# Prompt attention in another order of query blocks: 1, 8, 2, 7, 3, 6, 4, 5, with early and late blocks in pairs

## The chip, the core and the metric

The kernel runs on one core of one Trainium2 chip. The metric is the device time of one execution in microseconds (us). Five engines work side by side, each with a queue of its own in program order: TensorE (PE in the profile; its weight loads have a row of their own, PEld), VectorE (DVE), ScalarE (ACT), GpSimd (POOL) and SyncE (SP, which issues DMAs). They wait for one another by semaphores alone.

## The reference, cut to what matters

One layer of a streaming encoder: a SwiGLU feed-forward half step, a token mixer (a recurrent branch and an attention branch side by side), a second feed-forward half step and a final norm, for one prompt of 1024 tokens and eight running streams of 16 tokens. The change touches the attention of the prompt alone: 16 heads of width 64, causal, with a bias from summed forget gates.

```python
for blk in range(s_len // Q_BLOCK):                    # 8 blocks of 128 queries
    q0, q1 = blk * Q_BLOCK, (blk + 1) * Q_BLOCK
    s = einsum('bqhd,bkhd->bhqk', q[:, q0:q1], k[:, :q1]) * scale
    s = s + ft[:, :, q0:q1, None] - ft[:, :, None, :q1]
    p = softmax(where(causal, s, -inf))
    outs.append(einsum('bhqk,bkhd->bqhd', p, v[:, :q1]))
```

The n-th block of queries sees n blocks of 128 keys, so the eight blocks of a head have 1 to 8 key blocks, 36 in all. They do not depend on each other.

## The kernel before, in words

All matmuls that need float32 accuracy are done in a split form: a value is kept as a high part and a low part (the rest), and products of the parts are summed. In the prompt attention the probabilities are split into `pT_hi` and `pT_lo` (views of `w_hi` and `w_lo`), and the values tile `vs_[hh]` holds high and low columns beside each other, 128 in all.

Heads go in pairs: `PAIRS` = 8 rounds of a loop, each of 16 steps `k`, 8 for each of the two heads (`hh`). Step `k` handles query block `qi = k % 8`. Every engine has its own program for the same steps, written out by hand:

- **PE** (`att_tensor`), at step k: `scores` of step k+2 (L2212 and L2213, pieces of up to 512 keys against the high and the low part of k; then one 128-column matmul with the causal mask, L2214), into one of two score areas of two PSUM banks; `turn` of step k (L2227), which transposes the probabilities in units of up to four key blocks, one unit to a PSUM bank, banks 4 and 5 in turn; and half of `values` (L2246): in even steps the pass with `pT_hi`, in odd steps that with `pT_lo`, for the pair of query blocks that was finished by the step before. A pair of blocks (before: 2j and 2j+1) shares one output bank of 256 columns, so that a key block which both see is one matmul of 256 moving columns, and one that only the later block sees is one of 128 columns (`q0`).
- **DVE** (`att_vector`): `maxima` of step k+2 (L2419, adds the bias and takes the row extreme), `lows` of step k (L2435, a turned unit minus its high part, one for each unit), `output` (L2444, a pair's result to SBUF) and, at one step of a head, the reciprocal of the row sums (L2449) and its copy `rec_out` (L2424).
- **ACT** (`att_scalar`): `exp` of step k+1 (L2295), then the copies of step k's units to `pT_hi` (L2312); after step 1 of each head also `split_head_hi` (L2282, L2283), two copies of 1024 columns that round the next head's k and q.
- **POOL** (`att_gpsimd`): the low parts of the next head's k and q (L2334, L2337), the split of the values (L2346, L2348), and the sum, scaling and split of the finished heads (L2355, L2361, L2378, L2380).
- **SP** (`att_sync`): loads of k, q, v and bias for the heads to come, the store and reload of the inverse row sums, the move of one half of a head's output.

The waits that matter below: `turn` of a unit waits until the unit two before it has been read by `lows` (semaphore `pa_l`), since it overwrites that bank; it also waits for `exp` of its step (`pa_exp`). `scores` wait for `maxima` two steps earlier (`pa_max`), and at a head's first step for POOL's split (`pa_split`). `values` wait for the copies or lows of both blocks of the pair, and for `output` of the pair two before. The number of units before each step is a table, `UNITS_BEFORE`, and a head has 12 units in either order.

Of the kernel before, what the change touches and what calls it, by code (L numbers as in the profile page):

```python
# [58 lines left out]
def program(nc, ctx, a, o):  # L59
# [5 lines left out]
    def sem(name):  # L65
        if name not in S:
            S[name] = ctx.enter_context(nc.semaphore(name))
        return S[name]
# [2041 lines left out]
    PAIRS = H // 2  # L2110
    STEPS = 16
    QUARTERS = 8
    UNITS_BEFORE = (0, 1, 2, 3, 4, 6, 8, 10)
    HEAD_UNITS = 12
    vs_ = [v[:].rearrange("p (k n) -> p k n", n=128) for v in vs]
    pT_hi = [w[:].rearrange("p (k n) -> p k n", n=256) for w in w_hi[0:2]]
# [2 lines left out]
    def units_of(i, k):  # L2119

        first = i * 2 * HEAD_UNITS + (HEAD_UNITS * (k // 8) + UNITS_BEFORE[k % 8])
        return [(first + n, 4 * n, min(4 * n + 4, k % 8 + 1)) for n in range(k % 8 // 4 + 1)]

    def bank_of(k, n):
        return 4 + (UNITS_BEFORE[k % 8] + n) % 2
# [73 lines left out]
    def att_tensor(eng):  # L2199

        def scores(i, k):
            hh, qi = k // 8, k % 8
            keys = 128 * (qi + 1)
            if qi == 0:
                eng.wait_ge(sem("pa_split"), i * 2 + hh + 2)
            eng.wait_ge(sem("pa_max"), i * 16 + k - 2 + 1 + 16)
            lhs = q_hl[hh][:, 128 * qi:128 * qi + 128]
            for c0 in range(0, keys, 512):
                c1 = min(c0 + 512, keys)
                out = psum[:, 1024 * (k % 2) + c0:1024 * (k % 2) + c1]  # L2210

                eng.matmul(out, lhs, k_hi[hh][:, c0:c1], start=True, stop=False)  # L2212
                last = eng.matmul(out, lhs, k_lo[hh][:, c0:c1], start=False, stop=c1 < keys)  # L2213
            last = eng.matmul(psum[:, 1024 * (k % 2) + keys - 128:1024 * (k % 2) + keys], ident_r[:], causal_r[:],  # L2214
                              start=False, stop=True)
            last.then_inc(sem("pa_s"), 1)

        def turn(i, k, first):

            eng.wait_ge(sem("pa_exp"), i * 16 + k + 1)  # L2220
            for n, (e, k0, k1) in enumerate(units_of(i, k)):
                eng.wait_ge(sem("pa_l"), e - 1 + 2)
                if k == 10 or (k == 2 and not first):
                    eng.wait_ge(sem("pa_rec"), i * 2 + k // 10 + 2)
                    eng.transpose(ps[bank_of(k, n)][0:8, 384:512], srec[:, 1 - k // 10, :], ident[:])
                for kb in range(k0, k1):
                    last = eng.transpose(ps[bank_of(k, n)][:, 128 * (kb - k0):128 * (kb - k0) + 128],  # L2227
                                         pr[k % 4][:, 128 * kb:128 * kb + 128], ident[:])
                last.then_inc(sem("pa_t"), 1)

        def values(i, q, low):

            j, hh = q % 4, q // 4
            done = i * 2 * HEAD_UNITS + (HEAD_UNITS * hh + (UNITS_BEFORE + (HEAD_UNITS,))[2 * j + 2])
            if not low:
                if j == 0:
                    eng.wait_ge(sem("v_split"), i * 4 + 2 * hh + 2)
                eng.wait_ge(sem("pa_o"), i * 8 + q - 2 + 1 + 2)
                eng.wait_ge(sem("pa_h"), done)
            else:  # L2240
                eng.wait_ge(sem("pa_l"), done + 2)
            probs = (pT_lo if low else pT_hi)[q % 2]
            n = 2 * j + 2
            for kb in range(n):
                q0 = 128 if kb == n - 1 else 0
                last = eng.matmul(ps[6 + q % 2][:, q0:256], vs_[hh][:, kb, :], probs[:, kb, q0:256],  # L2246
                                  start=(not low and kb == 0), stop=(low and kb == n - 1))
            last.then_inc(sem("pa_vl" if low else "pa_vh"), 1)

        def body(i, first=False, last=False):  # L2250
            for k in range(STEPS):
                if k + 2 < STEPS:
                    scores(i, k + 2)
                elif not last:
                    scores(i + 1, k + 2 - STEPS)
                turn(i, k, first)
                if k >= 2:
                    values(i, (k - 2) // 2, k % 2 == 1)
                elif not first:
                    values(i - 1, QUARTERS - 1, k == 1)  # L2260

        eng.wait_ge(sem("br_free"), 20)
        scores(0, 0)
        eng.wait_ge(sem("br_free"), 22)
        scores(0, 1)
        eng.wait_ge(sem("br_free"), 24)
        eng.wait_ge(sem("state_out_ready"), 2)
        body(0, first=True)
        with eng.Fori(1, PAIRS - 1) as i:
            body(i)  # L2270
        body(PAIRS - 1, last=True)
        values(PAIRS - 1, QUARTERS - 1, False)
        values(PAIRS - 1, QUARTERS - 1, True)
        eng.wait_ge(sem("pa_rec"), 2 * PAIRS + 2)
        eng.wait_ge(sem("pa_l"), PAIRS * 2 * HEAD_UNITS + 2)
        eng.transpose(ps[4][0:8, 384:512], srec[:, 1, :], ident[:]).then_inc(sem("last_rec_turned"), 1)
# [8 lines left out]
    def att_scalar(eng):  # L2285
        eng.wait_ge(sem("br_full"), 24)
        eng.activation(acts_hi[:, :, TP:T], att_s[:], ACT.Copy).then_inc(sem("a_hi"), 1)

        def exp(i, k):
            hh, qi = k // 8, k % 8  # L2290
            keys = 128 * (qi + 1)
            if qi == 0:
                eng.wait_ge(sem("pa_rec"), i * 2 + hh - 1 + 2)
            eng.wait_ge(sem("pa_max"), i * 16 + k + 1 + 16)
            eng.activation(pr[k % 4][:, 0:keys], pr[k % 4][:, 0:keys], ACT.Exp, bias=stat[:, k % 4, 0:1], scale=-1.0,  # L2295
                           accum_out=ssum[:, hh, qi:qi + 1]).then_inc(sem("pa_exp"), 1)

        def body(i, first=False, last=False):
            if first:
                exp(i, 0)  # L2300
            for k in range(STEPS):
                if k + 1 < STEPS:
                    exp(i, k + 1)
                elif not last:
                    exp(i + 1, 0)
                hh, qi = k // 8, k % 8
                q = k // 2
                for n, (e, k0, k1) in enumerate(units_of(i, k)):
                    eng.wait_ge(sem("pa_t"), e + 1)
                    if not (first and q < 2):  # L2310
                        eng.wait_ge(sem("pa_vh"), i * 8 + q - 1)
                    eng.activation(pT_hi[q % 2][:, k0:k1, 128 * (qi % 2):128 * (qi % 2) + 128],  # L2312
                                   ps[bank_of(k, n)][:, 0:128 * (k1 - k0)].rearrange("p (k n) -> p k n", n=128),
                                   ACT.Copy).then_inc(sem("pa_h"), 1)
                if k == 1:
                    split_head_hi(eng, i, i * 2 + 1, 1)
                if k == 9 and not last:
                    split_head_hi(eng, i, i * 2 + 2, 0)
                if k == 13 and last:
                    eng.wait_ge(sem("v_split"), 4 * PAIRS)  # L2320
                    eng.wait_ge(sem("pa_s"), 16 * PAIRS + 16)
                    split_hi(eng, B_BRA, BRA_FIRST_SLOT, BRA_RAWS[0])
        body(0, first=True)
        with eng.Fori(1, PAIRS - 1) as i:
            body(i)
        body(PAIRS - 1, last=True)
        last = PAIRS - 1
        eng.wait_ge(sem("pair_scaled"), PAIRS + 1)
        eng.activation(acts_hi[:, last, 0:TP], lw[:], ACT.Copy).then_inc(sem("pair_hi"), 1)
# [74 lines left out]
    def att_vector(eng):  # L2404
# [5 lines left out]
        eng.wait_ge(sem("states_stored"), 64)  # L2410

        def maxima(i, k):
            hh, qi = k // 8, k % 8
            keys = 128 * (qi + 1)
            eng.wait_ge(sem("pa_s"), i * 16 + k + 1 + 16)
            if qi == 0:
                eng.wait_ge(sem(f"kbias_loaded{hh}"), i * 16 + 16)
            eng.memset(wait_marks[:, k % 4:k % 4 + 1], 0.0)
            eng.tensor_tensor_reduce(pr[k % 4][:, 0:keys], psum[:, 1024 * (k % 2):1024 * (k % 2) + keys],  # L2419
# [4 lines left out]
            eng.tensor_copy(rec_rows[:], bank[0:8, 384:512]).then_inc(sem("rec_moved"), 1)  # L2424

        def lows(i, k, first):
            qi, q = k % 8, k // 2
            for n, (e, k0, k1) in enumerate(units_of(i, k)):
                eng.wait_ge(sem("pa_h"), e + 1)
                if not (first and q < 2):  # L2430
                    eng.wait_ge(sem("pa_vl"), i * 8 + q - 1)
                if k == 10 or (k == 2 and not first):
                    rec_out(i * 2 + k // 10 - 1, ps[bank_of(k, n)])
                cols_ = slice(128 * (qi % 2), 128 * (qi % 2) + 128)
                eng.tensor_tensor(pT_lo[q % 2][:, k0:k1, cols_],  # L2435
                                  ps[bank_of(k, n)][:, 0:128 * (k1 - k0)].rearrange("p (k n) -> p k n", n=128),
                                  pT_hi[q % 2][:, k0:k1, cols_].bitcast(F32), ALU.subtract).then_inc(sem("pa_l"), 1)
# [1 line left out]
        def output(i, q, first=False):  # L2439
            hh, j = q // 4, q % 4  # L2440
            eng.wait_ge(sem("pa_vl"), i * 8 + q + 1)
            if j == 0 and not first:
                eng.wait_ge(sem("pair_added"), i * 2 + hh - 1)
            eng.tensor_copy(ou[hh][:, 256 * j:256 * j + 256], ps[6 + q % 2][:, 0:256]).then_inc(sem("pa_o"), 1)  # L2444

        def inverse(i, hh):
            hd = i * 2 + hh
# [320 lines left out]
```

## Time and profile before

| what | value |
|---|---|
| median of 3 runs | 3396.83 us (3395.95 to 3397.89) |
| the profiled execution | 3401.43 us, span of its instructions 3399.6 us |
| PE busy | 3269.5 us (96% of the span) |
| DVE, ACT, POOL busy | 1260.7, 986.6, 916.5 us |
| prompt attention, within the span | about 2046 to 2323 us |
| in it: PE, ACT, DVE, POOL busy | 242, 217, 212, 193 us of 277 |
| mean granted TensorE clock | 0.985 |

Starts are microseconds from the first instruction of the profiled execution. A row of a timeline gives the start, the duration, the engine, the source line, the operation, the output tile and the inputs, the shape, and how many instructions in a row were merged (x8); in square brackets how long the engine sat idle ahead of it, and who ended the wait. The starts of PE's matmuls and of its weight loads (PEld) are what the argument uses; the ends of matmuls are modelled.

### The profile page before, as it was taken

What the parts mean: (1) busy time and instruction counts of PE and PEld (TensorE: products, weight loads), DVE (VectorE), ACT (ScalarE), POOL (GpSimd) and SP (SyncE); (2) the same over time, 40 slices, a digit from 0 to 9 for tenths busy, and PEclk for the clock granted to TensorE, in tenths of its full rate; (3) what the DMA queues carried; (4) which work ended last, traced back from release to release, by engine and by line L of the source; (5) the groups of instructions that cost most, each with busy time, mean ns of one, the idle gap of its engine ahead of it and who ended that gap; (6) DMA issues with size and microseconds to landing.
All of it is one profiled execution on the core that took longest, in us unless ns stands there. A gap on an engine that the chain in (4) does not pass through costs nothing.

```text
span 3399.6 us, 53111 instructions
## 1 busy us (share of the span) xinstructions
PE 3269.5 (96%) x20617; PEld 3113.2 (92%) x20617; DVE 1260.7 (37%) x2587; ACT 986.6 (29%) x1577; POOL 916.5 (27%) x474
## 2 busy tenths in 40 slices
PE   7999999999998999999999998889999999999997
PEld 4899999999988999998877897879989999999997
DVE  5322222222267343541222316775343222333225
ACT  4111111111253233233434407873232111111114
POOL 2222222222331111111111025773133222322223
PEclk8999999999999999999999999999999999999999
DMA  6223222221121321326767745555211111111101
GB/s 220 87 95 102 89 87 98 86 88 60 38 83 35 113 84 63 107 77 230 265 213 270 258 138 136 139 140 177 96 38 63 37 37 37 37 49 37 58 17 56
DMA packets 247038, 351.80 MB, mean 103 GB/s; under 512 B 31885, under 2 KB 182981, under 8 KB 246658
## 3 DMA queue, kind: packets, MB, share of 16 engines
q1 hardware_dynamic: 220482, 316.87, 29.2%
q10 hardware_dynamic: 26432, 33.18, 2.7%
q8 instruction: 90, 1.47, 0.2%
q14 instruction: 34, 0.28, 0.0%
HBM read 297.74 MB, written 48.07 MB: 102 GB/s over the span
## 4 chain that ended last, share of the span: by engine, by line
PE 86%; DVE 5%; issue 3%; ACT 3%; SPq 1%; DMA 1%; POOL 1%; ACTq 0%; DVEq 0%; POOLq 0%
PE psum L304 25%; PE psum L308 25%; PE psum L307 25%; PE psum L1753 2%; PE psum L2227 1%; PE psum L489 1%; PE psum L2246 1%; PE psum L1800 1%; DVE w_lo L2435 1%; PE psum L1394 1%; PE psum L1767 1%; DVE acts_lo L830 1%; DVE h_f L785 1%; PE psum L496 1%; PE psum L2212 1%
## 5 line engine op out<-in xcount | busy, mean ns | idle before, releaser
L304 PE MATMUL psum<-acts_hi,w_hi 128*128 128x384 f32 x4032 | 1392.9, 345 | 10.8 <-issue 9.2
L308 PE MATMUL psum<-acts_hi,w_lo 128*128 128x384 f32 x4032 | 1357.6, 337 | 0.0
L307 PE MATMUL psum<-acts_lo,w_hi 128*128 128x384 f32 x4032 | 1357.2, 337 | 0.0
L304 PEld LDWEIGHTS psum<-acts_hi,w_hi 128*128 128x128 f32 x4032 | 760.4, 189 | 48.4 <-issue 31.2
L294 POOL TENSOR_TENSOR w_lo<-w_raw,w_hi 128x2048 fp32r<-128x2048 f32 x106 | 491.0, 4639 | 1148.1 <-ACT w_hi L288 1148.1
L307 PEld LDWEIGHTS psum<-acts_lo,w_hi 128*128 128x128 f32 x4032 | 760.7, 189 | 4.4 <-issue 0.9
L308 PEld LDWEIGHTS psum<-acts_hi,w_lo 128*128 128x128 f32 x4032 | 759.5, 188 | 0.0
L1116 DVE TENSOR_TENSOR u_f<-psum,gated 128x384 f32<-128x384 f32 x132 | 73.6, 558 | 1014.5 <-ACT gated L1010 1014.5
L1066 POOL TENSOR_TENSOR u_lo<-u_f,u_hi 128x384 fp32r<-128x384 f32 x132 | 134.4, 1018 | 928.5 <-ACT u_hi L1015 928.5
L1188 DVE SCALAR_TENSOR_TENSOR x<-psum,mods,x 128x384 f32<-128x384 f32 (+1 forms) x552 | 314.6, 570 | 183.7 <-PE psum L308 183.7
L288 ACT ACTIVATE w_hi<-w_raw 128x2048 fp32r<-128x2048 f32 x106 | 200.5, 1910 | 560.7 <-PE psum L304 535.1
L304 PE MATMUL psum<-u_hi,w_hi 128*128 128x384 f32 x1056 | 356.3, 337 | 3.4 <-DVE x L1193 2.2
L308 PE MATMUL psum<-u_hi,w_lo 128*128 128x384 f32 x1056 | 355.6, 337 | 0.0
L307 PE MATMUL psum<-u_lo,w_hi 128*128 128x384 f32 x1056 | 355.5, 337 | 0.0
L1010 ACT ACTIVATE gated<-psum 128x384 f32<-128x384 f32 x132 | 64.8, 491 | 892.7 <-PE psum L308 892.6
L304 PEld LDWEIGHTS psum<-u_hi,w_hi 128*128 128x128 f32 x1056 | 199.0, 188 | 4.9 <-DVE x L1193 3.3
L307 PEld LDWEIGHTS psum<-u_lo,w_hi 128*128 128x128 f32 x1056 | 198.9, 188 | 0.3
L308 PEld LDWEIGHTS psum<-u_hi,w_lo 128*128 128x128 f32 x1056 | 199.1, 189 | 0.0
L1967 DVE COPY kTs<-psum 128x512 f32<-128x512 f32 x64 | 44.3, 692 | 251.1 <-PE psum L1753 251.1
L2227 PE MATMUL psum<-ident,pr 128*128 128x128 f32 x576 | 92.8, 284 | 32.0 <-DVE w_lo L2435 27.8
L2435 DVE TENSOR_TENSOR w_lo<-psum,w_hi 128x512 fp32r<-128x512 f32 (+1 forms) x192 | 100.4, 551 | 27.3 <-ACT w_hi L2312 26.5
L2227 PEld LDWEIGHTS psum<-ident,pr 128*128 128x128 f32 x576 | 63.3, 142 | 46.8 <-DVE w_lo L2435 29.8
(261 smaller groups left out, 2978.7 us busy)
## 6 DMA issues: line engine op xcount, KB each, us to landing
w_raw<-in_ffn_w SPq DMA_DIRECT2D x66, 1024.0 KB, 5.2
kc<-in_cache_k SPq DMA_DIRECT2D x32, 1024.0 KB, 7.0
vc<-in_cache_v SPq DMA_DIRECT2D x16, 2048.0 KB, 7.9
w_raw<-in_w_ada SPq DMA_DIRECT2D x28, 1024.0 KB, 5.0
w_raw<-in_w_in SPq DMA_DIRECT2D x28, 1024.0 KB, 5.1
sp<-sample_bias SPq DMA_DIRECT2D x128, 65.0 KB, 2.6
ada_w<-in_w_ada SPq DMA_DIRECT2D x4, 2048.0 KB, 13.4
w_raw<-in_w_ada_f SPq DMA_DIRECT2D x8, 1024.0 KB, 5.7
```

The costliest lines, as they stand in the source:

```text
L288: eng.activation(w_hi[st][:], w_raw[raw][:], ACT.Copy).then_inc(sem("w_hi_done"), 1)
L294: eng.tensor_tensor(w_lo[st][:], w_raw[raw][:], w_hi[st][:].bitcast(F32), ALU.subtract).then_inc(sem("w_lo_done"), 1)
L304: pass1 = eng.matmul(out, whi, ahi, start=first, stop=False)
L307: eng.matmul(out, whi, alo, start=False, stop=False)
L308: return eng.matmul(out, wlo, ahi, start=False, stop=last)
L1010: eng.activation(gated[n % 2][:], ps[2 * (n % 2)][:, 0:CH], ACT.Silu).then_inc(sem("gated_ready"), 1)
L1066: eng.tensor_tensor(u_lo[:, t, tokens_of(c)], u_f[n % 2][:], u_hi[:, t, tokens_of(c)].bitcast(F32), ALU.subtract).then_inc(sem("u_lo_done" ...
L1116: eng.tensor_tensor(u_f[n % 2][:], ps[2 * (n % 2) + 1][:, 0:CH], gated[n % 2][:], ALU.mult).then_inc(sem("u_free"), 1)
L1188: last = eng.scalar_tensor_tensor(xt[:, d, t0:t0 + cp], bank[:, 0:cp], mods[:, gate, d, 0:1], xt[:, d, t0:t0 + cp], ALU.mult, ALU.add)
L1753: last = eng.transpose(ps[TURNED][:, 128 * m:128 * m + 128], kc[:, 4 * half + m, 128 * p:128 * p + 128], ident[:])
L2227: last = eng.transpose(ps[bank_of(k, n)][:, 128 * (kb - k0):128 * (kb - k0) + 128], pr[k % 4][:, 128 * kb:128 * kb + 128], ident[:])
L2435: eng.tensor_tensor(pT_lo[q % 2][:, k0:k1, cols_], ps[bank_of(k, n)][:, 0:128 * (k1 - k0)].rearrange("p (k n) -> p k n", n=128), pT_hi[q % ...
```

## The change

`BLOCKS` gives the query block of each of a head's eight steps: 0, 7, 1, 6, 2, 5, 3, 4 (counted from 0). Two steps in a row are a pair, now an early and a late block: 1 and 8 key blocks, 2 and 7, 3 and 6, 4 and 5. `UNITS_BEFORE` follows from the order. In `values` the key blocks that both see are those up to the early block; all further ones are matmuls of 128 columns. `output` writes its two blocks to two separate places. The number of steps, of units, of transposes, of score matmuls and the positions of all other work in the steps stay. The diff, without lines that only rename an index:

```diff
-    UNITS_BEFORE = (0, 1, 2, 3, 4, 6, 8, 10)
+    BLOCKS = (0, 7, 1, 6, 2, 5, 3, 4)
+    UNITS_BEFORE = tuple(sum(qi // 4 + 1 for qi in BLOCKS[:n]) for n in range(8))
...
-        return [(first + n, 4 * n, min(4 * n + 4, k % 8 + 1)) for n in range(k % 8 // 4 + 1)]
+        qi = BLOCKS[k % 8]
+        return [(first + n, 4 * n, min(4 * n + 4, qi + 1)) for n in range(qi // 4 + 1)]
...
         def scores(i, k):
-            hh, qi = k // 8, k % 8
+            hh, qi = k // 8, BLOCKS[k % 8]
             keys = 128 * (qi + 1)
-            if qi == 0:
+            if k % 8 == 0:
                 eng.wait_ge(sem("pa_split"), i * 2 + hh + 2)
...
             probs = (pT_lo if low else pT_hi)[q % 2]
-            n = 2 * j + 2
+            early, late = BLOCKS[2 * j], BLOCKS[2 * j + 1]
+            n = late + 1
             for kb in range(n):
-                q0 = 128 if kb == n - 1 else 0
+                q0 = 128 if kb > early else 0
                 last = eng.matmul(ps[6 + q % 2][:, q0:256], vs_[hh][:, kb, :], probs[:, kb, q0:256],
                                   start=(not low and kb == 0), stop=(low and kb == n - 1))
...
         def exp(i, k):
-            hh, qi = k // 8, k % 8
+            hh, qi = k // 8, BLOCKS[k % 8]
...
         def maxima(i, k):
-            hh, qi = k // 8, k % 8
+            hh, qi = k // 8, BLOCKS[k % 8]
...
-            eng.tensor_copy(ou[hh][:, 256 * j:256 * j + 256], ps[6 + q % 2][:, 0:256]).then_inc(sem("pa_o"), 1)
+            early, late = BLOCKS[2 * j], BLOCKS[2 * j + 1]
+            out = ou[hh][:].rearrange("p (b n) -> p b n", n=128)[:, early:late + 1:late - early, :]
+            eng.tensor_copy(out, ps[6 + q % 2][:, 0:256].rearrange("p (b n) -> p b n", n=128)).then_inc(sem("pa_o"), 1)
```

## Rows read from the trace of the kernel before

**Rows 1.** Busy us (count) of PE, PEld, DVE, ACT, POOL by stretch; granted clock, DMA.

```profile
2046.00:2323.00 277.00, 242.23 (x1744) 219.15 (x1745) 212.24 (x672) 216.83 (x480) 192.65 (x98) 0.98 0.54 129
...
2323.00:2700.00 377.00, 368.17 (x2083) 365.70 (x2082) 147.35 (x262) 81.93 (x121) 112.25 (x52) 0.99 0.26 87
```

**Rows 2.** Timeline of PE's matmuls in one head and the start of the next.

```profile
2182.17 0.98 PE L2227 MATMUL psum<-ident,pr 128*128 128x128 f32 x7 [0.65 <-DVE w_lo L2435]
...
2191.80 0.65 PE L2227 MATMUL psum<-ident,pr 128*128 128x128 f32 x4
...
2194.80 0.33 PE L2227 MATMUL psum<-ident,pr 128*128 128x128 f32 x1 [0.82 <-DVE w_lo L2435]
...
2198.84 0.98 PE L2227 MATMUL psum<-ident,pr 128*128 128x128 f32 x7 [0.66 <-DVE w_lo L2435]
```

**Rows 3.** Who waited for whom, 2084 to 2300 us: total, times, longest.

```profile
PEld psum L2227 <- DVE w_lo L2435: 28.4, 37, 1.1
...
PEld psum L2227 <- issue: 3.0, 14, 0.8
```

**Rows 4.** Instructions by line and shape, 1900 to 2700 us: count, busy us, mean ns.

```profile
L2246 PE MATMUL psum<-w_lo,vs 128*128 128x256 f32 x256 | 46.3, 303 | 0.0
...
L2246 PE MATMUL psum<-w_lo,vs 128*128 128x128 f32 x64 | 14.4, 224 | 0.0
```

**Rows 5.** Timeline of PE's weight loads, one for each matmul.

```profile
2181.07 0.19 PEld L2213 LDWEIGHTS psum<-k_lo,q_hl 128*128 128x128 f32 x1
2181.18 0.19 PEld L2214 LDWEIGHTS psum<-causal_r,ident_r 128*128 128x128 f32 x1
...
2184.41 0.89 PEld L2227 LDWEIGHTS psum<-ident,pr 128*128 128x128 f32 x8 [0.40 <-DVE w_lo L2435]
...
2186.48 0.14 PEld L2227 LDWEIGHTS psum<-ident,pr 128*128 128x128 f32 x1
2186.68 1.01 PEld L2246 LDWEIGHTS psum<-w_hi,vs 128*128 128x128 f32 x8
```

**Rows 6.** PE's matmuls in one scores piece, behind a piece of 512 columns.

```profile
2189.66 0.40 PE L2213 MATMUL psum<-k_lo,q_hl 128*128 128x512 f32 x1
2189.90 0.22 PE L2212 MATMUL psum<-k_hi,q_hl 128*128 128x128 f32 x1
2189.95 0.27 PE L2213 MATMUL psum<-k_lo,q_hl 128*128 128x128 f32 x1
```

**Rows 7.** Timeline of ACT: two copies of a step, then the split stretch.

```profile
2182.94 0.98 ACT L2312 ACTIVATE w_hi<-psum 128x512 fp32r<-128x512 f32 x2 [0.15 <-PE psum L2227]
...
2188.97 1.05 ACT L2282 ACTIVATE k_hi<-kf 128x1024 fp32r<-128x1024 f32 x1
...
2190.86 0.71 ACT L2295 ACTIVATE pr<-pr,stat 128x512 f32<-128x512 f32 x1
...
2191.57 0.48 ACT L2312 ACTIVATE w_hi<-psum 128x384 fp32r<-128x384 f32 x1
```

**Rows 8.** Timeline of DVE, the low part of the same step.

```profile
2192.39 0.54 DVE L2435 TENSOR_TENSOR w_lo<-psum,w_hi 128x384 fp32r<-128x384 f32 x1
```

**Rows 9.** Instructions by line and shape again, of ACT and DVE.

```profile
L2435 DVE TENSOR_TENSOR w_lo<-psum,w_hi 128x512 fp32r<-128x512 f32 x96 | 64.5, 686 | 22.1 <-ACT w_hi L2312 21.5
...
L2312 ACT ACTIVATE w_hi<-psum 128x512 fp32r<-128x512 f32 x96 | 55.3, 593 | 21.3 <-PE psum L2227 20.8
...
L2295 ACT ACTIVATE pr<-pr,stat 128x896 f32<-128x896 f32 x16 | 16.7, 1046 | 0.0
```

**Rows 10.** Whole timeline: POOL's q split, and scores of the next head.

```profile
2193.51 2.38 POOL L2337 TENSOR_TENSOR q_hl<-qf,q_hl 64x1024 fp32r<-64x1024 f32 x1
...
2197.69 0.27 PE L2212 MATMUL psum<-k_hi,q_hl 128*128 128x128 f32 x1
```

**Rows 11.** Timeline of PE at the last two steps of the last head.

```profile
2314.58 0.95 PE L2227 MATMUL psum<-ident,pr 128*128 128x128 f32 x7 [1.02 <-DVE w_lo L2435]
...
2318.11 1.06 PE L2227 MATMUL psum<-ident,pr 128*128 128x128 f32 x8 [1.93 <-DVE w_lo L2435]
```

More of the change, by code:

```diff
@@ L2289, in exp @@
         def exp(i, k):
-            hh, qi = k // 8, k % 8
+            hh, qi = k // 8, BLOCKS[k % 8]
             keys = 128 * (qi + 1)
-            if qi == 0:
+            if k % 8 == 0:
                 eng.wait_ge(sem("pa_rec"), i * 2 + hh - 1 + 2)
@@ L2311, in body @@
                         eng.wait_ge(sem("pa_vh"), i * 8 + q - 1)
-                    eng.activation(pT_hi[q % 2][:, k0:k1, 128 * (qi % 2):128 * (qi % 2) + 128],
+                    eng.activation(pT_hi[q % 2][:, k0:k1, 128 * (k % 2):128 * (k % 2) + 128],
                                    ps[bank_of(k, n)][:, 0:128 * (k1 - k0)].rearrange("p (k n) -> p k n", n=128),
@@ L2412, in maxima @@
         def maxima(i, k):
-            hh, qi = k // 8, k % 8
+            hh, qi = k // 8, BLOCKS[k % 8]
             keys = 128 * (qi + 1)
             eng.wait_ge(sem("pa_s"), i * 16 + k + 1 + 16)
-            if qi == 0:
+            if k % 8 == 0:
                 eng.wait_ge(sem(f"kbias_loaded{hh}"), i * 16 + 16)
@@ L2426, in lows @@
         def lows(i, k, first):
-            qi, q = k % 8, k // 2
+            q = k // 2
             for n, (e, k0, k1) in enumerate(units_of(i, k)):
@@ L2433, in lows @@
                     rec_out(i * 2 + k // 10 - 1, ps[bank_of(k, n)])
-                cols_ = slice(128 * (qi % 2), 128 * (qi % 2) + 128)
+                cols_ = slice(128 * (k % 2), 128 * (k % 2) + 128)
                 eng.tensor_tensor(pT_lo[q % 2][:, k0:k1, cols_],
```

## The prediction

> **What bounds the kernel now.** I read the busy times by stretch first, then the prompt attention alone. TensorE works nearly without a break in the stretches around it, 368 of 377 us in the one that follows, but 242 of 277 us within it [rows 1]; whatever the attention gains or loses is thus passed on to the end. The granted clock is 0.98 there and 0.99 in the next stretch, both near the level of 2.4 GHz [rows 1], so it plays no part. PE's timeline is periodic: the same seven transposes begin at 2182.17 and at 2198.84, so a head takes 16.67 us [rows 2]. The waits of the weight loads, PE's front edge, say how much of this is idle: 28.4 us for DVE's `lows` and 3.0 us for what the profile calls issue, in 216 us [rows 3]. That is 31.4 / 216 x 16.67 = 2.42 us for a head. The rest, 14.25 us, is work in program order. The longest waits, 0.65 to 0.82 us, are where PE wants a turned bank (4 or 5) that DVE has not read yet [rows 2]. DVE and ACT are busy for 212 and 217 of 277 us [rows 1]: no engine is full, PE is nearest to it, and the gaps come from round trips PE, ACT, DVE, PE.
>
> The new order can win at most those 2.42 us a head, 38.7 us over 16 heads, less what it adds.
>
> **What it adds: six more matmuls in each pass.** Before, the pairs have 2, 4, 6 and 8 key blocks; one pass over a head is 16 matmuls of 256 columns and 4 of 128, as the counts 256 and 64 over 16 heads say [rows 4]. After, the pairs have 8, 7, 6 and 5 key blocks, of which 1, 2, 3 and 4 are shared: 10 of 256 columns and 16 of 128. The columns are the same, 16 x 256 + 4 x 128 = 10 x 256 + 16 x 128 = 4608; the matmuls, and with them the weight loads, go from 20 to 26.
>
> Which of the two is paid? Eight value matmuls load their weights within 1.01 us, the last load of 0.19 included, so one follows the next after 0.82 / 7 = 0.117 us. Two loads for 128-column matmuls in a row (2181.07, 2181.18) stand 0.11 us apart [rows 5]. So halving the columns saves 0.007 us, not half. A 128-column matmul starts 0.05 us behind another only where the one ahead of both was long (2189.66, 2189.90, 2189.95) and the weights were there early [rows 6]; a long run of them is nearer to the first case. With 0.11: before 16 x 0.117 + 4 x 0.11 = 2.31 us a pass, after 10 x 0.117 + 16 x 0.11 = 2.93. That is 0.62 a pass, 1.24 a head (two passes), 19.8 us in all. The lower bound is 0, if columns alone counted; the upper one is 6 x 0.117 x 2 x 16 = 22.5 us.
>
> The Trainium skill (TensorE: Matmul & The Clock Gate, LDWEIGHTS) gives a weight load's time as its columns over 1.2, 107 ns for 128, whatever the rows; the 0.11 us agree, and by this rule the change costs PE time. Another rule of that page (Back-to-back issue gap) puts a stream of load and matmul pairs at 81 ns for 128 columns, against the 0.11 measured here; by it the added work, with 12 more such matmuls in each of two passes, would be 1.24 - 24 x 0.03 = 0.52 us a head.
>
> **What it moves: where PE waits.** Prices first. Four transposes: the eight loads of 0.89 less a single one of 0.14, over 7, give 0.107 each, 0.43 for four [rows 5]. Scores: a 512-column piece takes 0.24 (2189.66 to 2189.90), so 0.06 a block, at least 0.11 a matmul, twice for high and low, and 0.11 for the mask [rows 5, 6]: 0.33, 0.35, 0.47, 0.59, 0.81, 0.83, 0.95 us for 1 to 7 blocks. Passes after: 0.89, 0.78, 0.68, 0.58 for 8, 7, 6, 5 blocks. A bank's round trip: the first half of the seven transposes ends at 2182.17 + 0.43 = 2182.60, and the bank is used again at 2184.41, 1.81 us later [rows 2, 5]; its pieces, 0.34 to the copy, 0.59, 0.69 and some 0.05 of handing over, make 1.67 [rows 7, 9].
>
> Units now come 1, 2, 1, 2, ... by step. I walked one head through and compared, at each place where PE needs something, PE's own work since then with the time until it is there. Four places are not covered.
>
> (A) Step 3. After the first half of block 8 is turned (step 1), ACT needs 0.34 to begin, 0.98 for two copies, 1.89 for the split of the next head (2188.97 to 2190.86), then `exp` of seven key blocks, 0.71 + (1.046 - 0.713) = 1.04, and 0.23 until PE begins (2191.57 to 2191.80) [rows 2, 7, 9]: 4.48 us. PE has the other half 0.43, the 5-block pass 0.58, scores of 3 blocks 0.47, the turn of step 2 with the inverse 0.32, the 8-block pass 0.89, scores of 6 blocks 0.83: 3.52. It waits 0.96. Before, ACT had one copy ahead of the split at this place, and an `exp` of four blocks behind it.
>
> (B) Step 3, second half. Its bank frees when step 2's copy and low part are done, which stand behind that `exp` on ACT. Before, copy, inverse and low part took from 2191.57 to 2192.39 + 0.54, 1.36 us for three blocks [rows 7, 8]; for two about 1.15 (an estimate: two instructions a block shorter, 0.1 each). PE arrives after 0.23 + 0.43: a wait of 0.49.
>
> (C) Step 6. Covered: 0.21 + 0.78 + 0.33 = 1.32 of a bank's trip. DVE is free there, so 1.67 is taken: 0.35, at most 0.49.
>
> (D) Step 0 of the next head. Covered: 0.11 + 0.68 + 0.35 = 1.14; DVE has `maxima` of block 8 ahead of the second half, so 1.81 is taken: 0.67, at least 0.53.
>
> Together 2.47 us (2.33 to 2.61) in place of 2.42. The waits do not go, they move. So a head grows by 1.24 + 0.05 = 1.29 us, 16 heads by 20.6. The ends give back about 1: the last head waits 1.02 and 1.93 us behind ACT's weight split today [rows 11], and its last `exp` has five blocks instead of eight, 3 x 0.11 less; the start, one long scores piece earlier, I bound by 1 us either way.
>
> **Edits at no cost.** `maxima`, `exp`, copies and `lows` have the same shapes and counts a head. `output` still moves 256 columns, on DVE, which has room. The waits that moved from `qi == 0` to `k % 8 == 0` guard the same steps. SP's and POOL's instructions keep their places. The split starts later in a head, after two copies and eight blocks: 0.11 + 0.58 + 0.95 + 0.43 + 0.34 + 0.98 = 3.39 us from the head's first turn against 2.49 before (2186.48 to 2188.97) [rows 5, 7]. POOL's low part of q ended at 2195.89, 1.8 us ahead of the next head's scores [rows 10]; these come 11.2 us after the head's first turn today, and after the change 12.6: scores of 7, 3, 6, 4 and 5 blocks 3.65, 27 blocks turned and the inverse 3.00, six passes 4.50, (A) and (B) 1.45. So the slack grows by 0.5; if this cover went, each us would cost 16.
>
> **The sum.** On the profiled execution, 3401.43 us (span 3399.6), +20.6 - 1 = 3421; it stood 4.6 above the median of the runs, so 3396.8 + 19 = 3416 us.
>
> **Rivals.** (1) The evening-out works and the bank waits go, as a pair of steps now weighs the same wherever it stands; for it speaks that ACT and DVE have a fifth of their time free, against it the 0.96 us of (A), a sum of ACT work in queue order. It decides where a head's waits fall below 2.42 - 1.24 = 1.18 us; with none left the time is (1.24 - 2.42) x 16 = -19: 3378. Chance 0.09. (2) Waits fall by half and pay for the loads, within 0.2% (6.8 us, about what a measurement of this kernel can tell from no change): 3390 to 3403, 0.10. (3) Matmuls of 128 columns run at 0.06: no work added, but where PE's work covered a trip the wait takes it back, 0.05 for each of 1 + 7 in (A), 5 in (C), 3 in (D), 0.8 us. A head grows by 0.85, in all 13 less 1: 3409. Against it stands the 0.11; 0.08. With the 81 ns of the Trainium skill's page (TensorE: Matmul & The Clock Gate, Back-to-back issue gap) the same reckoning gives 0.52 + 0.05 + 0.48 = 1.05 a head, 3413. (4) POOL's split comes late after all, 1 us a head on top: 3432, 0.03. The forecast itself has 0.70, with 3405 to 3426.
>
> Slower: 0.70 + 0.08 + 0.03 = 0.81; same 0.10; faster 0.09. The range is 3400 to 3428: the forecast's own, case 3, and half of case 2; upward the longest trips (2.61 for 2.47, +2) and loads at 0.117 (+3), with as much again for places that I missed.
>
> **What would show it.** The period of a head near 18 us instead of 16.67; 160 matmuls of 256 and 256 of 128 columns in the low pass, 0.11 apart; waits of the turn's weight loads near 2.4 us a head, the longest at step 3, behind `exp`, none on scores for POOL. Wrong would be it if the loads of 128-column matmuls stand closer, or if the wait behind ACT's split does not appear.

## The result, and the profile after

The changed kernel takes 3407.49 us (median of 9), the kernel before 3398.51 in the runs beside it: a ratio of 1.0029, 95% interval 1.002 to 1.0038. A second series gave 3409.63 and 1.0028 (1.0018 to 1.0038). So it is slower, by 9 to 11 us, where 19 were forecast. The time lies in the range, and just beyond the 0.2% that the prediction took as no change.

The period of a head is read from the reciprocal of its row sums, which DVE computes once in each head. Two such rows, ten heads apart, in the timeline of DVE, kernel before:

```profile
2121.23 0.19 DVE L2449 RECIPROCAL srec<-ssum 128x8 f32<-128x8 f32 x1
...
2288.10 0.19 DVE L2449 RECIPROCAL srec<-ssum 128x8 f32<-128x8 f32 x1
```

And after:

```profile
2119.80 0.19 DVE L2453 RECIPROCAL srec<-ssum 128x8 f32<-128x8 f32 x1
...
2295.89 0.19 DVE L2453 RECIPROCAL srec<-ssum 128x8 f32<-128x8 f32 x1
```

That is 16.69 us a head before and 17.61 after, 0.92 more; the prediction had 1.29. A second profile of each kernel gave 16.69 and 17.61 again.

Value matmuls by shape, after, as in [rows 4]:

```profile
L2249 PE MATMUL psum<-w_lo,vs 128*128 128x128 f32 x256 | 35.7, 262 | 0.0
...
L2249 PE MATMUL psum<-w_lo,vs 128*128 128x256 f32 x160 | 34.7, 315 | 0.0
```

The waits of the turn's weight loads, 2084 to 2310 us, as in [rows 3]:

```profile
PEld psum L2229 <- DVE w_lo L2437: 17.0, 36, 0.6
...
PEld psum L2229 <- issue: 8.8, 15, 0.7
...
PEld psum L2227 <- issue: 1.7, 7, 0.3
...
PEld psum L2227 <- DVE w_lo L2437: 1.1, 6, 0.2
```

Together 28.6 us in 226, 2.23 us a head, against 2.42 before (a single wait for `exp`, 0.6 us after and 0.3 before, is left out of both). The rest of a head is 15.38 us against 14.27.

One head in PE's timeline, after, as in [rows 2], from step 0 to step 3:

```profile
2188.83 0.33 PE L2229 MATMUL psum<-ident,pr 128*128 128x128 f32 x1 [0.43 <-DVE w_lo L2437]
2189.03 0.80 PE L2249 MATMUL psum<-w_hi,vs 128*128 128x256 f32 x5
2189.66 0.45 PE L2214 MATMUL psum<-k_hi,q_hl 128*128 128x512 f32 x1
...
2193.02 1.08 PE L2249 MATMUL psum<-w_hi,vs 128*128 128x256 f32 x8
2193.94 0.45 PE L2214 MATMUL psum<-k_hi,q_hl 128*128 128x512 f32 x1
...
2195.36 0.65 PE L2229 MATMUL psum<-ident,pr 128*128 128x128 f32 x4 [0.45 <-ACT pr L2298]
2196.31 0.55 PE L2229 MATMUL psum<-ident,pr 128*128 128x128 f32 x3 [0.30 <-DVE w_lo L2437]
```

The weight loads of the same head, whose waits are PE's front edge, with the eight loads of the 8-block pass:

```profile
2188.82 0.14 PEld L2229 LDWEIGHTS psum<-ident,pr 128*128 128x128 f32 x1 [0.58 <-DVE w_lo L2437]
...
2192.68 0.08 PEld L2227 LDWEIGHTS psum<-ident,srec 128*8 128x8 f32 x1 [0.26 <-issue]
...
2192.99 0.97 PEld L2249 LDWEIGHTS psum<-w_hi,vs 128*128 128x128 f32 x8
...
2195.35 0.42 PEld L2229 LDWEIGHTS psum<-ident,pr 128*128 128x128 f32 x4 [0.59 <-issue]
...
2196.31 0.31 PEld L2229 LDWEIGHTS psum<-ident,pr 128*128 128x128 f32 x3 [0.54 <-DVE w_lo L2437]
...
2202.10 0.42 PEld L2229 LDWEIGHTS psum<-ident,pr 128*128 128x128 f32 x4 [0.25 <-DVE w_lo L2437]
```

All four places of the prediction are there: (D) at 2188.82, (A) at 2195.35, (B) at 2196.31, (C) at 2202.10. A fifth is new: 0.26 us at step 2 (2192.68), inside the stretch over which (A) was counted. Together they make 2.22 us.

ACT in the same stretch: two copies of block 8, the split, `exp` of seven blocks, and only then the copy of step 2:

```profile
2191.23 1.09 ACT L2314 ACTIVATE w_hi<-psum 128x512 fp32r<-128x512 f32 x2 [1.14 <-PE psum L2229]
2192.21 1.06 ACT L2285 ACTIVATE k_hi<-kf 128x1024 fp32r<-128x1024 f32 x1
2193.16 1.06 ACT L2286 ACTIVATE q_hl<-qf 128x1024 fp32r<-128x1024 f32 x1
2194.10 1.04 ACT L2298 ACTIVATE pr<-pr,stat 128x896 f32<-128x896 f32 x1
...
2195.13 0.38 ACT L2314 ACTIVATE w_hi<-psum 128x256 fp32r<-128x256 f32 x1
```

And DVE, which waits 2 us for that copy:

```profile
2195.65 0.28 DVE L2426 COPY rec_rows<-psum 8x128 f32<-8x128 f32 x1 [2.00 <-ACT w_hi L2314]
2195.85 0.40 DVE L2437 TENSOR_TENSOR w_lo<-psum,w_hi 128x256 fp32r<-128x256 f32 x1
```

So the profile looks as forecast, a little smaller. What it cannot say is whether the head is longer for the loads or for the order: the prediction put 1.24 of its 1.29 us on the loads.

### The profile page after: what moved, and what is told of

Its sections match the earlier page's. It is cut to its first block, busy times and chain, and to the rows that moved or that the text cites. A ratio compares the mean times of both kernels' runs of the same rounds, so it can differ in the third digit from the quotient of the medians.

```text
span 3404.5 us, 53491 instructions
## 1 busy us (share of the span) xinstructions
PE 3285.7 (97%) x20809; PEld 3128.6 (92%) x20809; DVE 1260.8 (37%) x2587; ACT 986.3 (29%) x1577; POOL 916.7 (27%) x474
## 4 chain that ended last, share of the span: by engine, by line
PE 88%; DVE 5%; ACT 3%; issue 1%; SPq 1%; DMA 1%; POOL 1%; ACTq 0%; DVEq 0%; POOLq 0%
PE psum L304 25%; PE psum L308 25%; PE psum L307 25%; PE psum L2249 2%; PE psum L2229 2%; PE psum L1753 2%; PE psum L489 1%; PE psum L1800 1%; PE psum L1394 1%; PE psum L1767 1%; DVE acts_lo L830 1%; PE psum L2214 1%; DVE w_lo L2437 1%; PE psum L2215 1%; DVE h_f L785 1%
## 5 line engine op out<-in xcount | busy, mean ns | idle before, releaser
L2437 DVE TENSOR_TENSOR w_lo<-psum,w_hi 128x128 fp32r<-128x128 f32 (+2 forms) x192 | 100.6, 550 | 35.7 <-ACT w_hi L2314 35.2
L2314 ACT ACTIVATE w_hi<-psum 128x128 fp32r<-128x128 f32 (+2 forms) x192 | 88.8, 488 | 62.6 <-PE psum L2229 62.6
```

Source lines behind the costliest of these rows:

```text
L2314: eng.activation(pT_hi[q % 2][:, k0:k1, 128 * (k % 2):128 * (k % 2) + 128], ps[bank_of(k, n)][:, 0:128 * (k1 - k0)].rearrange("p (k n) -> ...
L2437: eng.tensor_tensor(pT_lo[q % 2][:, k0:k1, cols_], ps[bank_of(k, n)][:, 0:128 * (k1 - k0)].rearrange("p (k n) -> p k n", n=128), pT_hi[q % ...
```

## The experiments

All times are medians beside runs of the kernel before on the same chip; a head is the mean over ten heads, read as above.

| kernel | us | ratio to before (95%) | a head, us |
|---|---|---|---|
| g1_before_again (the kernel before) | 3399.25 | 1.0001 (0.9992 to 1.0010) | 16.69 |
| g2_after_again (the changed kernel) | 3409.63 | 1.0028 (1.0018 to 1.0038) | 17.61 |
| e1_cut | 3400.32 | 1.0005 (0.9996 to 1.0014) | 16.93 |
| e2_fewer | 3403.84 | 1.0018 (1.0009 to 1.0027) | 17.27 |
| e3_new_split0 | 3404.76 | 1.0018 (1.0009 to 1.0027) | 16.97 |
| e4_old_split0 | 3388.23 | 0.9973 (0.9962 to 0.9983) | 15.99 |
| f1_old_split0_late | 3388.68 | 0.9968 (0.9956 to 0.9981) | 15.99 |
| f2_new_split0_late | 3399.90 | 1.0004 (0.9995 to 1.0013) | 16.98 |
| f3_new_split0_fewer | 3394.00 | 0.9986 (0.9977 to 0.9995) | 16.40 |
| f4_order_0213 | 3387.05 | 0.9967 (0.9954 to 0.9979) | 15.74 |
| g3_old_split0_cut | 3393.81 | 0.9986 (0.9977 to 0.9995) | 16.44 |

Two theories stand against each other. L: the six further matmuls of a pass are paid wherever they stand. W: PE works into waits for a bank or for ACT, so that added work costs little, and the order costs by its waits.

**The loads alone (e1_cut).**

```diff
-            for kb in range(n):
-                q0 = 128 if kb == n - 1 else 0
+            halved = range(1, 1 + (0, 2, 2, 2)[j])
+            for kb in range(n):
+                parts = [(128, 256)] if kb == n - 1 else [(0, 128), (128, 256)] if kb in halved else [(0, 256)]
+                for q0, q1 in parts:
...
```

> The old order, with six of the 256-column value matmuls of each pass cut into two of 128 (two in each of the three longer pairs): 26 matmuls a pass, 10 of 256 and 16 of 128 columns, as in the changed kernel. Nothing else changes. Theory L (the loads are the cost, wherever they stand): a head grows by 1.24 us, the kernel by 19 to 20 us, as after the change or more. Theory W (what PE gets to do while a bank's trip is open anyway costs little): a pass of the long pairs stands right ahead of the waits for a bank, so most of it is hidden; a head grows by 0.3 us, from 16.69 to about 17.0, the kernel by 5 us, and the waits for the bank fall by 0.9 us a head.

The timeline of DVE and the waits of this kernel, 2090 to 2300 us:

```profile
2117.84 0.19 DVE L2451 RECIPROCAL srec<-ssum 128x8 f32<-128x8 f32 x1
...
2287.09 0.20 DVE L2451 RECIPROCAL srec<-ssum 128x8 f32<-128x8 f32 x1
```

```profile
PEld psum L2227 <- DVE w_lo L2437: 21.9, 37, 1.1
PEld psum L2227 <- issue: 0.5, 1, 0.5
```

A head grows by 0.24 us of the 1.24, the kernel by 2 us, which the interval does not tell from nothing. The waits fall from 2.42 to 22.4 / 210 x 16.93 = 1.81 us a head. Theory L is out for the old order: there the loads are mostly hidden.

**The order alone (e2_fewer).**

```diff
-            n = late + 1
+            n = late + 1 - (2, 2, 1, 1)[j]
```

> The new order and pairs, but each pass leaves out its last six 128-column matmuls (two in the first and second pair, one in the third and fourth), so that it has 20 matmuls as before; the last key blocks do not enter the output. Theory L: a head gets back 1.3 us, the kernel stands about 10 us under the kernel before. Theory W: the waits for ACT and for the banks take up most of what is left out, a head gets back only 0.35 to 0.4 us (17.6 to about 17.2), and the kernel stays some 3 us above the kernel before: the order itself, without a single load more, is then the slower one.

Its reciprocals and its waits:

```profile
2120.36 0.19 DVE L2453 RECIPROCAL srec<-ssum 128x8 f32<-128x8 f32 x1
...
2293.03 0.19 DVE L2453 RECIPROCAL srec<-ssum 128x8 f32<-128x8 f32 x1
```

```profile
PEld psum L2229 <- DVE w_lo L2437: 26.2, 48, 0.8
PEld psum L2229 <- issue: 11.3, 13, 0.9
PEld psum L2227 <- issue: 2.1, 6, 0.4
PEld psum L2227 <- DVE w_lo L2437: 1.8, 6, 0.3
```

Without one matmul more than before, and with six blocks of 128 columns fewer in each pass, a head takes 17.27 us: 0.58 of the 0.92 us come from the order. The waits rise to 41.4 / 210 x 17.27 = 3.40 us a head. With the loads back in (the changed kernel) they are 2.23: the loads fill 1.17 us of waits and lengthen the head by 0.34.

The traces also show what the work itself took. From the start of a pass's first matmul to the start of the matmul behind the pass, the eight passes of a head take together 4.93 us before, 6.19 after, 6.18 in e1_cut and 4.95 in e2_fewer (means over the same ten heads). So the six matmuls a pass cost PE their 1.25 us a head in either order; what differs is how much of this falls into time in which PE would have waited. The waits as read do not balance the growth of the head to better than 0.4 us (0.61 and 0.24 in e1_cut, 1.17 and 0.34 here, against 1.25).

**ACT's split at another step.** In the changed kernel (e3_new_split0) and in the kernel before (e4_old_split0):

```diff
-                if k == 1:
+                if k == 0:
                     split_head_hi(eng, i, i * 2 + 1, 1)
-                if k == 9 and not last:
+                if k == 8 and not last:
                     split_head_hi(eng, i, i * 2 + 2, 0)
```

> The changed kernel, with ACT's split of the next head's k and q after step 0's copies instead of step 1's; so it no longer stands between block 8's copies and the exp of block 7. If the wait (A) of the prediction comes from that chain, the wait before step 3's turn goes, and a head shrinks by 0.5 us, the kernel by 8 to 9 us against the changed one, to about the time of the kernel before. If the waits at step 3 have another cause, or only move on to another step, nothing changes within 0.1 us a head.

> The kernel before, with the same move of ACT's split alone (after step 0's copies). Theory W: in the old order too the split delays exp and with it the maxima and the turned banks behind it; a head shrinks by 0.7 us, the kernel by 10 to 12 us. Theory L has nothing for this move: PE's work stays, so no change.

Reciprocals of e3_new_split0, then of e4_old_split0:

```profile
2124.35 0.19 DVE L2453 RECIPROCAL srec<-ssum 128x8 f32<-128x8 f32 x1
...
2294.01 0.19 DVE L2453 RECIPROCAL srec<-ssum 128x8 f32<-128x8 f32 x1
```

```profile
2120.48 0.19 DVE L2449 RECIPROCAL srec<-ssum 128x8 f32<-128x8 f32 x1
...
2280.39 0.19 DVE L2449 RECIPROCAL srec<-ssum 128x8 f32<-128x8 f32 x1
```

The heads shrink by 0.64 us in the new order and by 0.70 in the old one, as W had it. The kernel before gains 10 us by this move alone. The changed kernel got 3 us only, not 8 or 9: its first head was longer (32.6 us from the first scores to the first reciprocal, against 27.4). In the old order the waits from 2036 to 2090 us show that ACT came too early for a load of k and q there:

```profile
ACT k_hi L2282 <- DMA qf<-q_t: 4.4, 1, 4.4
```

So both were run once more with the first head's split left at step 1 (`if k == (1 if first else 0)`).

> The old order with ACT's split after step 0's copies, but in the first head still after step 1's: there the split at step 0 waited 4.4 us for the loads of k and q. Expected: the first head gets its 2.5 us back, the others stay at 16.0 us; the kernel 2 to 3 us under the run with the move in every head, about 12 us under the kernel before. If ACT's wait in the first head was hidden, no change against that run.

> The new order with the same move, the first head kept at step 1. The heads stay at 17.0 us, the first one gets back about 5 us: the kernel 8 us under the changed one, within 2 us of the kernel before. If the move in every head won only 3 us for another reason than the first head's loads, it stays there.

The new order gained the 5 us and is level with the kernel before. The old one gained nothing (3388.68 against 3388.23), against the expectation. Its profile shows 1.3 us won at the start (29.2 us to the first reciprocal instead of 30.5) and 1.2 lost at the end (18.6 us from the last reciprocal but one to the merge instead of 17.4), where the granted clock was 0.91 instead of 1.00. That is one profile of each kernel; whether the timed runs had it too is open. In f2_new_split0_late, the rows of PE's timeline in steps 2 and 3 are these:

```profile
2191.22 0.27 PE L2227 MATMUL psum<-ident,srec 128*8 128x128 f32 x1 [0.76 <-DVE w_lo L2437]
...
2193.29 0.94 PE L2229 MATMUL psum<-ident,pr 128*128 128x128 f32 x7
```

Step 3 no longer waits: (A) and (B) are gone, and their cause is the split ahead of `exp`. But step 2 now waits 0.76 us for the bank of the first half of block 8, where its weight loads waited 0.26 in the changed kernel. Part of the gain turned into that wait.

**Loads and waits once more.** With the split moved, the loads were left out of the new order (f3_new_split0_fewer) and put into the old one (g3_old_split0_cut), by the edits above.

> The same as the run ahead of it, and each pass leaves out its last six 128-column matmuls (the last key blocks do not enter the output). Where the split stood at step 1, leaving them out won 0.34 us a head of their 1.24. If what hid the rest was the wait behind ACT's split, more of it comes out now: 0.6 us a head, 17.0 to 16.4 to 16.5, the kernel 8 to 10 us under the run ahead. If the loads count little in any case, 0.3 us a head again, 5 us.

> The old order with the split after step 0's copies (first head step 1) and with six value matmuls a pass cut in two, so 26 a pass. With the split at step 1 this cut cost 0.24 us a head of 1.24. With fewer waits left to hide it (2.53 instead of 3.17 us a head) it costs more: 0.4 to 0.5 us a head, 16.0 to about 16.45, 6 to 8 us against the uncut one. If it costs 0.24 again, the waits that hide it are not those that the split made.

Reciprocals of f3_new_split0_fewer, then of g3_old_split0_cut:

```profile
2120.99 0.19 DVE L2453 RECIPROCAL srec<-ssum 128x8 f32<-128x8 f32 x1
...
2285.01 0.19 DVE L2453 RECIPROCAL srec<-ssum 128x8 f32<-128x8 f32 x1
```

```profile
2118.53 0.19 DVE L2451 RECIPROCAL srec<-ssum 128x8 f32<-128x8 f32 x1
...
2282.94 0.19 DVE L2451 RECIPROCAL srec<-ssum 128x8 f32<-128x8 f32 x1
```

Six matmuls more a pass cost 0.24 us a head in the old order and 0.34 in the new one; with the split moved, 0.45 (15.99 to 16.44) and 0.58 (16.40 to 16.98). In each order the price of the same work rises as the waits around it go. Their sum alone does not set it: without these matmuls the new order had 3.40 us of waits a head and the old one 2.42, yet the new one paid more. (The 3.17 and 2.53 us in the expectation of g3_old_split0_cut are near the whole idle time of the weight loads, not the waits of the turn alone.)

The kernel's time moved by 5 to 6 us for both. For f3_new_split0_fewer 8 to 10 were expected. One early head of its profile was 2.4 us longer than the rest: in it ACT waited 0.9 us for a load of q, PE then 1.9 us for a bank, and the granted clock was 0.91, against 1.00 in the heads beside it. Whether the timed runs had such a head is open.

**A milder mixing (f4_order_0213).** `BLOCKS = (0, 2, 1, 3, 4, 5, 6, 7)` in the changed kernel's code, the split as in f2_new_split0_late.

> The changed kernel's code with the order 1, 3, 2, 4, 5, 6, 7, 8 (pairs 1 and 3, 2 and 4, the long ones as before the change: one matmul more a pass than before) and ACT's split as in the runs ahead. A small mixing of the short blocks alone, with few loads more: a head of 15.8 us against 16.0 in the old order with the split moved, 2 to 4 us under that run. If any early and late mixing only adds waits, it is slower than that run.

```profile
2115.01 0.20 DVE L2453 RECIPROCAL srec<-ssum 128x8 f32<-128x8 f32 x1
...
2272.45 0.19 DVE L2453 RECIPROCAL srec<-ssum 128x8 f32<-128x8 f32 x1
```

A head takes 15.74 us, 0.25 less than in the old order with the same split. The kernel's 3387.05 us are the lowest of all, 0.33% under the kernel before (0.21 to 0.46%); its lead of 1.6 us over f1_old_split0_late is within the scatter of the runs.

**Both kernels again.**

> The kernel before once more, for a second profile of it. In the first profiles the attention grew by 12.0 us from before to after, the time by 9. If the attention of before takes 278.6 us again (first scores to the first matmul of the merge), the 3 us lie in the stretches around it; if it takes about 281 us, the first profile's attention was a short one.

> The changed kernel once more, for a second profile and more timed runs: heads of 17.6 us again, the attention 290 us, the time 9 us above the kernel before.

From the first scores to the first matmul of the merge, the kernel before took 278.6 us in its first profile and 280.7 in the second, the changed one 290.5 and 290.6. So the attention grew by 9.9 to 12.0 us. The heads were the same in both profiles; what differed was the start and the end, where before's first profile was short and had the higher granted clock (the last section shows the end). The 9 to 11 us of the timed runs agree with that.

## Why the prediction was right in sign and half off in size

- **What bounds the kernel: right.** What the attention gained or lost came out at the end, in each run to within 4 us (its length in the run's profile against the mean of the two profiles before, 279.6 us).
- **The price of the loads: right as work.** The starts after give 0.92 us for the 8-block pass (2193.02 to 2193.94) and 0.63 for the 5-block one (2189.03 to 2189.66), where 0.89 and 0.58 were forecast; all passes of a head grew by 1.26 us, where 1.24 were. Counts are 256 and 160, as forecast. In a pass, the first 128-column matmul was followed after 0.06 us, as in [rows 6], the others after 0.11; the loads of the value passes never stood closer than 0.108 us in these ten heads (2192.99: 0.97 less the last load of 0.19, over 7, is 0.111). So rival (3) is out. The Trainium skill (TensorE: Matmul & The Clock Gate, Back-to-back issue gap) has a stream of load and matmul pairs at 81 ns for 128 columns; the loads here stood further apart, and the measurement decides.
- **What part of the price reaches the head: wrong, the step that failed.** The sum took 1.24 us a head as added in full, and the order as nearly free (+0.05). The runs show the reverse: the order alone +0.58, the loads on top +0.34 (or, the other way round, the loads alone +0.24 and the order on top +0.68). The walk had its waits at (A) to (D) right as places, but it counted them with the loads already in place and set them against the 2.42 us of the old order; the growth was then read off as "the loads". With the loads left out, the waits are 3.40 us. As a mere balance the sum came nearer: 1.11 us more work and 0.19 us less waiting, where 1.24 more and 0.05 more were forecast. That the time fell in the range is in part luck: 3407 lies nearest to the 3409 of rival (3), whose mechanism is out.
- **The size of a head: too large, 1.29 for 0.92.** The waits came to 2.23 us instead of 2.47: (A) 0.59 and the 0.26 of step 2 within its stretch, for 0.96; (B) 0.54 for 0.49; (C) 0.25 for 0.35; (D) 0.58 for 0.67. The rest of the head grew by 1.11 instead of 1.24. Times 16 this is 5.9 us of the miss. (The prediction's "longest waits, 0.65 to 0.82 us" are PE's in the head shown; those of the weight loads reach 1.1 [rows 3].)
- **The ends: too small.** With 16 x 0.92 = 14.7 us from the heads, the attention grew by 9.9 to 12.0: the ends gave back 3 to 5 us, not 1. The last interval between reciprocals went from 16.05 to 14.92 us; against the 0.92 more that the sum adds for this head too, that gives back 2.0, where the prediction had 1. A term was missing there: the last head has no next one to split for (`k == 9 and not last`), so (A) and (B), 1.45 us in the walk, do not arise in it. Its step 3 in the changed kernel, in PE's timeline:

```profile
2317.89 0.95 PE L2229 MATMUL psum<-ident,pr 128*128 128x128 f32 x7
```

No wait stands ahead of these seven transposes. The same trace thus shows once more that the split causes (A) and (B). The first head (first scores to first reciprocal 28.0 and 29.1 us before, 27.4 and 27.5 after) gave back 1.6 to 2.5 by the same count, where the prediction allowed 1 either way. The granted clock there was 0.82 and 0.77 before and 0.88 after in both profiles; the prediction went by the mean of 0.98 [rows 1] and gave the clock no part. How much of the start is the clock's no run separates.

- **Rival (1), the evening-out: wrong.** (A), the ACT work in queue order, is what it would have had to beat. Moving the split showed it: without (A) the new order comes level with the unmoved old one, but the old order gains as much by the same move.
- **Rival (4), POOL: out.** No wait of scores for the split appears among PE's waits after.

## What to carry to other kernels

Work added to the busiest engine costs only what its waits do not take in; here the same matmuls cost 0.24 to 0.58 of their 1.24 us a head, depending on the waits around them. So price an edit by what stands behind each wait, and test its parts one by one, before the sum is put down to the part that is easiest to count. Before an order is changed, look for the lump of work in a queue that makes the order matter: one split, moved ahead by a step, won 10 us in the old order, where the new order with the split in its old place lost 9 to 11. And look at the first and the last round of a loop by themselves: a lump that is missing in one of them changes what that round gains.

## What the runs showed of the hardware that was not expected

The granted clock falls to its lower level, 1.2 GHz, for a few microseconds in some executions and not in others, behind the same wait of the same code. In the stretch from 1900 to 1920 us, ahead of the attention, PE waits 2.17 us for a copy in the kernel before and 2.18 in the changed one. The busy times and granted clock (0.91 and 1.00) of the two are:

```profile
1900.00:1920.00 20.00, 17.40 (x159) 14.38 (x160) 4.30 (x9) 9.04 (x12) 2.83 (x1) 0.91 0.42 147
```

```profile
1900.00:1920.00 20.00, 17.14 (x171) 13.68 (x171) 4.14 (x9) 9.07 (x13) 4.59 (x1) 1.00 0.53 176
```

The difference of 0.09 over 20 us is 1.8 us of full clock, for nothing in the change; in the changed kernel's second profile that stretch had 0.91 too.

The end of the attention shows the same, from the last reciprocal but one to the first weight matmul of the merge. These are the two profiles of the kernel before; in both PE waits 1.02 and 1.93 us there, as in [rows 11]:

```profile
2304.56:2321.95 17.39, 14.09 (x108) 12.87 (x107) 11.81 (x33) 11.97 (x24) 9.65 (x4) 1.00 0.12 31
```

```profile
2303.89:2322.43 18.54, 15.42 (x108) 14.31 (x107) 11.80 (x33) 11.96 (x24) 9.67 (x4) 0.91 0.11 29
```

That is 1.15 us more at the lower mean clock, in one and the same kernel. In the ten heads by which the periods are read, the granted clock was 1.00 in every profile. Effects of two or three microseconds in this kernel are thus read from the period of a head, not from the span.
